# Latent attention in four quarters of four heads, woven between the projections of the next quarter

## The reference

```python
def mla(h, w_in, q_norm, w_q_up, kv_norm, w_kv_up, w_o):
    B, S, _ = h.shape
    lat = h @ w_in                                   # 384 + 256 + 32 columns
    cq = lat[..., :Q_LORA]
    ckv = lat[..., Q_LORA:Q_LORA + KV_LORA]
    k_rope = lat[..., Q_LORA + KV_LORA:][:, :, None, :]
    q = (rmsnorm(cq, q_norm) @ w_q_up).reshape(B, S, MLA_HEADS, QK_NOPE + QK_ROPE)    # 16 heads of 64 + 32
    kv = (rmsnorm(ckv, kv_norm) @ w_kv_up).reshape(B, S, MLA_HEADS, QK_NOPE + V_HEAD) # 16 heads of 64 + 64
    pos = jnp.arange(S, dtype=jnp.float32)
    q = jnp.concatenate([q[..., :QK_NOPE], rope(q[..., QK_NOPE:], pos)], axis=-1)
    k_rope = jnp.broadcast_to(rope(k_rope, pos), (B, S, MLA_HEADS, QK_ROPE))
    k = jnp.concatenate([kv[..., :QK_NOPE], k_rope.astype(kv.dtype)], axis=-1)
    v = kv[..., QK_NOPE:]
    o = causal_block_attention(q, k, v, (QK_NOPE + QK_ROPE) ** -0.5)
    return o.reshape(B, S, MLA_HEADS * V_HEAD) @ w_o
```

## Time and profile before

| what | value |
|---|---|
| median of 3 runs | 4606.94 us (4595.18 to 4607.84) |
| profiled execution, its time and span | 4603.62 us, 4601.8 us |
| TensorE busy | 4149.3 us, 90% of the span |
| VectorE, ScalarE, GpSimd busy | 50%, 28%, 18% |
| granted TensorE clock, mean | 0.91 |
| chain that ended last | PE 84%, DVE 11%, ACT 3%, issue 2% |

### The profile page before, as it was taken

The page is one execution under the profiler, slowest core; times in us unless marked ns, Lnnn a source line. Parts: engine busy times, 40 slices in busy tenths (PEclk is TensorE's granted clock), DMA queues, the critical chain, the costliest instruction groups (busy, mean ns, idle before and its releaser), DMA issues.

```text
span 4601.8 us, 50066 instructions
## 1 busy us (share of the span) xinstructions
PE 4149.3 (90%) x20156; PEld 3325.7 (72%) x20156; DVE 2298.0 (50%) x3067; ACT 1278.5 (28%) x1698; POOL 848.2 (18%) x580
## 2 busy tenths in 40 slices
PE   6885799997759999999877899999999999999998
PEld 5744688885457887888644788878877777777886
DVE  4546555564565555555354543453354444445334
ACT  3231223222313223222333322232233232232222
POOL 2300244541004554565201220000000000000000
PEclk8877899996869999999778899989989999998999
DMA  4200144430004444454101233323322121112331
GB/s 141 83 1 1 55 137 142 147 123 28 1 1 124 138 149 126 138 148 133 53 14 42 55 96 92 92 80 94 101 65 76 60 72 51 62 49 64 101 92 64
DMA packets 538850, 378.37 MB, mean 82 GB/s; under 512 B 8938, under 2 KB 536267, under 8 KB 538619
## 3 DMA queue, kind: packets, MB, share of 16 engines
q1 hardware_dynamic: 538042, 373.07, 27.3%
q10 hardware_dynamic: 576, 2.10, 0.1%
HBM read 372.96 MB, written 2.17 MB: 82 GB/s over the span
## 4 chain that ended last, share of the span: by engine, by line
PE 84%; DVE 11%; ACT 3%; issue 2%; SPq 0%; DMA 0%; DVEq 0%; ACTq 0%
PE bank L433 55%; PE bank L477 6%; PE bank L755 3%; PE bank L447 3%; PE bank L775 3%; PE bank L535 2%; PE bank L1204 2%; DVE w_lo L412 2%; PE bank L1598 1%; PE bank L1623 1%; PE bank L765 1%; DVE hgrn_scores L1137 1%; ACT w_hi L403 1%; PE bank L1643 1%; PE bank L554 1%
## 5 line engine op out<-in xcount | busy, mean ns | idle before, releaser
L433 PE MATMUL bank<-H_hi,w_hi 128*128 128x512 f32 (+1 forms) x2368 | 955.3, 403 | 6.1 <-DVE w_lo L412 5.9
L412 DVE TENSOR_TENSOR w_lo<-w_raw,w_hi 128x2048 fp32r<-128x2048 f32 (+2 forms) x281 | 730.2, 2599 | 439.3 <-ACT w_hi L403 432.5
L433 PE MATMUL bank<-H_lo,w_hi 128*128 128x512 f32 (+1 forms) x2368 | 927.1, 392 | 0.0
L433 PE MATMUL bank<-H_hi,w_lo 128*128 128x512 f32 (+1 forms) x2368 | 926.5, 391 | 0.0
L403 ACT ACTIVATE w_hi<-w_raw 128x2048 fp32r<-128x2048 f32 (+2 forms) x281 | 528.3, 1880 | 321.0 <-DMA w_raw<-in_ffn_w_up 148.4
L433 PE MATMUL bank<-U_hi,w_hi 128*128 128x512 f32 x1440 | 568.2, 395 | 8.2 <-DVE U_lo L1188 6.1
L433 PE MATMUL bank<-U_lo,w_hi 128*128 128x512 f32 x1440 | 563.3, 391 | 0.0
L433 PE MATMUL bank<-U_hi,w_lo 128*128 128x512 f32 x1440 | 562.6, 391 | 0.0
L433 PEld LDWEIGHTS bank<-H_hi,w_hi 128*128 128x128 f32 (+1 forms) x2368 | 446.4, 189 | 117.7 <-issue 21.5
L433 PEld LDWEIGHTS bank<-H_hi,w_lo 128*128 128x128 f32 (+1 forms) x2368 | 446.1, 188 | 96.2
L433 PEld LDWEIGHTS bank<-H_lo,w_hi 128*128 128x128 f32 (+1 forms) x2368 | 446.9, 189 | 89.4 <-issue 3.9
(11 more groups left out here) (288 smaller groups left out, 5319.8 us busy)
## 6 DMA issues: line engine op xcount, KB each, us to landing
w_mod_raw<-in_w_mod SPq DMA_DIRECT2D x144, 512.0 KB, 6.3
w_raw<-in_ffn_w_gate SPq DMA_DIRECT2D x88, 512.0 KB, 3.9
w_raw<-in_ffn_w_up SPq DMA_DIRECT2D x88, 512.0 KB, 5.2
w_raw<-in_dil_w_in SPq DMA_DIRECT2D x36, 1024.0 KB, 4.9
w_raw<-in_w_mlp_in SPq DMA_DIRECT2D x32, 1024.0 KB, 6.3
w_raw<-in_w_mlp_out SPq DMA_DIRECT2D x32, 1024.0 KB, 5.4
w_raw<-in_ffn_w_down SPq DMA_DIRECT2D x32, 1024.0 KB, 5.2
w_raw<-in_w_in SPq DMA_DIRECT2D x16, 1024.0 KB, 5.3
```

The costliest lines, as they stand in the source:

```text
L412: dve.eng.tensor_tensor(WL[u % SLOTS][:, 0:n], RAW[u % SLOTS][:, 0:n], WH[u % SLOTS][:, 0:n].bitcast(F32), ALU.subtract).then_inc(lo_done. ...
L433: mm = pe.eng.matmul(bank[0:m, :], w[:, k, c0:c0 + m], r[:, k, :], start=(k == 0 and i == 0), stop=(k == kt - 1 and i == 2))
```

## The change

The sixteen heads are done in four quarters of four heads. The weights of a quarter are loaded by head parts, with the 64 plain features of its four heads together and then the 32 rotated ones (or the values), so a query unit has three tiles of 128 rows (two with plain features of two heads each, one with the rotated features of four heads), and a key/value unit two tiles of keys and two of values (256 columns for each of two blocks of tokens). The rotation works on that tile of four heads at once: one swap product and two multiplications of 128 rows, and four additions into the four heads' query tiles.

An item may now hold several blocks of queries in one bank: a head has three items, of blocks 0 and 2 (128 + 384 keys), 3 (512) and 1 (256). The barriers are gone. In `mla_pe` the quarters' projections (two units) have 17 points, three projection products apart (six of 256 columns for the values), at which the attention steps of the quarter before, the norm and rotation of the keys (in the first quarter) and the query rotation (point 12) are issued; the last quarter's attention stands at 18 points in mla_out's first two units. All three engines walk through the same list of points; ScalarE takes projections out at the points of `MLA_EVACS`, and both splits of the unit two ahead stand at points 8 and 16. The query latents are normed inside mla_in's third unit. Banks 0 to 2 take the projections' sums; bank 3 holds the heads' results. The other attentions keep their order, with the steps in functions of their own.

```diff
-    for base in (0, 64):
+    for base in (0, 32, 64, 96):
...
+        def add_units(stage, rhs, specs, waits="tiles", acc=(0, 1, 2, 3)):
...
+                for part in range(4):
+                    q = wq[:, 4 * QK * part:4 * QK * (part + 1)].rearrange("r (h c) -> r h c", c=QK)
+                    kv = wkv[:, 4 * P * part:4 * P * (part + 1)].rearrange("r (h c) -> r h c", c=P)
+                    add_units(("mla_q", part), cq, [([(0, q[:, :, 0:NOPE]), (4 * NOPE, q[:, :, NOPE:QK])], 3, 4 * QK,
+                                                     [feat(0, P), feat(P, P), feat(2 * P, P)])], "none" if part else "tiles", acc=(0, 1, 2))
+                    add_units(("mla_kv", part), ckv, [([(0, kv[:, :, 0:NOPE]), (4 * NOPE, kv[:, :, NOPE:P])], 2, 4 * P,
+                                                       [feat(0, P), feat(P, P), tok(2 * P, 2 * P, [0, 1]), tok(2 * P, 2 * P, [2, 3])])],
+                              "none" if part else "tiles", acc=(0, 1, 2))
+                add_units(("mla_out",), U, [square(io["mla_w_o_2"][0], D, 256 * n) for n in range(4)])
...
+        def pe_pair(pe, u, weave=None, beside=4):
...
+            for together in (todo[:beside],) + ((todo[beside:],) if beside < 4 else ()):
+                for _, _, _, place, turn in together:
+                    pe.eng.wait_ge(acc_free[place].sem, turn - 1)
+                for k in range(kt):
+                    if together[0] is todo[0]:
+                        pe.eng.wait_ge(rhs_ready.sem, rhs_ready.next(pe))
...
+        def mla_slot(h):
+            return (h + 4) % 8
...
+        def mla_items(part):
+            items = []
+            for h in range(4 * part, 4 * part + 4):
+                s = mla_slot(h)
+                stat = 0
+                for blocks in ((0, 2), (3,), (1,)):
+                    segs, vals, c0 = [], [], 0
+                    for b in blocks:
+                        w = (b + 1) * P
+                        segs.append((MQ[0:QK, s, b * P:(b + 1) * P], MK[0:QK, s, 0:w], c0, CAUSAL))
+                        vals += [(MV[:, kb, s * HEAD:(s + 1) * HEAD], b * P, kb == 0, kb == b) for kb in range(b + 1)]
+                        c0 += w
+                    items.append({"segs": segs, "n": c0, "scale": QK ** -0.5, "stat": h * NB + stat, "row": HEAD * (h % 2), "v": vals,
+                                  "opens": h % 2 == 0 and blocks[0] == 0, "closes": h // 2 if h % 2 == 1 and blocks[0] == 1 else None})
+                    stat += len(blocks)
+            return items
...
+        MLA_POINTS = 17
+
+        def mla_steps(part):
+            if part == 0:
+                return []
+            n, out = 12, []
+            for s in range(n + 2):
+                if s < n:
+                    out.append(("scores", s))
+                if 1 <= s < n + 1:
+                    out += [("divide", s - 1), ("turn", s - 1)]
+                if s >= 2:
+                    out.append(("values", s - 2))
+            return out
+
+        def mla_at(part, points=MLA_POINTS):
+            todo = mla_steps(part)
+            where = [[] for _ in range(points)]
+            for j, step in enumerate(todo):
+                where[(2 * j + 1) * points // (2 * len(todo))].append(step)
+            if part == 0:
+                where[1].append(("latent_sums", 0))
+                where[4].append(("latent_spread", 0))
+                where[6].append(("key_swap", 0))
+                where[9].append(("key_rows", 0))
+            if part < 4:
+                where[12].append(("query_rope", part))
+            return where
+
+        MLA_EVACS = {2: ("mla_q", 0), 5: ("mla_q", 1), 8: ("mla_q", 2), 10: ("mla_kv", 0), 12: ("mla_kv", 1), 14: ("mla_kv", 2), 16: ("mla_kv", 3)}
...
+            elif kind == "query_rope":
+                sem, n = mla_last(("mla_q", part), 0, 2)
+                pe.eng.wait_ge(sem, n)
+                pe.eng.wait_ge(turn_used.sem, turn_used.next(pe, lag=1))
+                pe.eng.wait_ge(pt_ready.sem, pt_ready.taken["pe"])
+                pe.eng.matmul(banks[6][:], MSWAP, MR[:], start=True, stop=True).then_inc(turn_mm.sem, turn_mm.add())
+            else:
+                if kind == "scores" and i == 0:
+                    pe.eng.wait_ge(mla_ready.sem, mla_ready.next(pe))
+                    sem, n = mla_last(("mla_kv", part - 1), 0, 3)
+                    pe.eng.wait_ge(sem, n)
+                    if part == 1:
+                        pe.eng.wait_ge(key_rows.sem, key_rows.next(pe, 8))
+                if kind == "turn":
...
+        def mla_pe(pe):
+            first = lin[("mla_in",)][0]
+            pe_pair(pe, first)
+            beside = iter([None] * 5 + ["sums"] + [None] * 4 + ["spread"] + [None] * 5)
+
+            def latents():
+                what = next(beside)
+                if what == "sums":
+                    pe_sums(pe, 3, NT[0:2])
+                elif what == "spread":
+                    pe_spread(pe)
+            pe_unit(pe, first + 2, latents)
+            for part in range(5):
+                items = mla_items(part - 1) if part else []
+                where = iter(mla_at(part, MLA_POINTS if part < 4 else 18))
+
+                def weave():
+                    for step in next(where):
+                        mla_pe_step(pe, part, items, step)
+                if part < 4:
+                    pe_unit(pe, lin[("mla_q", part)][0], weave)
+                    pe_unit(pe, lin[("mla_kv", part)][0], weave)
+                else:
+                    pe_pair(pe, lin[("mla_out",)][0], weave, 3)
+                    for u in lin[("mla_out",)][2:]:
+                        pe_unit(pe, u)
...
+        def mla_act(act):
...
+            for part in range(5):
+                items = mla_items(part - 1) if part else []
+                for p, steps_ in enumerate(mla_at(part, MLA_POINTS if part < 4 else 18)):
+                    if part < 4 and p in MLA_EVACS:
+                        stage, j = MLA_EVACS[p]
+                        mla_evac(act, part, stage, j)
+                        if p in (8, 16):
...
+                if part == 0:
+                    act.eng.wait_ge(mla_rows.sem, mla_rows.next(act))
+                    for h in range(8):
+                        ae.activation(MK[NOPE:QK, h, :], MK0[NOPE:QK, :], ACT.Copy).then_inc(key_rows.sem, key_rows.add())
+                        act.eng.wait_ge(key_rows.sem, key_rows.made)
...
+            elif kind == "query_rope":
...
+                ve.tensor_tensor(MT[0][:], MR[:], COS[:], ALU.mult).then_inc(dve.step.sem, dve.step.add())
...
+                ve.tensor_tensor(MT[1][:], banks[6][:], SIN[:], ALU.mult).then_inc(turn_used.sem, turn_used.add())
...
+                for j in range(4):
+                    r = slice(ROPE * j, ROPE * j + ROPE)
+                    signal = mla_ready if j == 3 else dve.step
+                    ve.tensor_tensor(MQ[NOPE:QK, s + j, :], MT[0][r, :], MT[1][r, :], ALU.add).then_inc(signal.sem, signal.add())
+                    dve.eng.wait_ge(signal.sem, signal.made)
...
+                    if part < 4 and p in (8, 16):
+                        split_lo(dve, lin[(MLA_EVACS[p][0], part)][0] + AHEAD)
+                    for step in steps_:
...
+                    if len(src.shape) == 3:
+                        h, w = src.shape[1:]
+                        for k in range(kt):
+                            eng.dma_start(dst[:, k, c:c + h * w].rearrange("p (h w) -> p h w", w=w), src[k * P:(k + 1) * P]).then_inc(landed[s].sem, landed[s].add(16))
+                        continue
```

413 lines of the change are left out of this document (191 added, 222 removed).

## The result

The changed kernel took 4576.06 us (median of 5 runs), the kernel before beside it 4601.12 us (5 runs). The ratio is 0.9934, 95% interval 0.9922 to 0.9947: 24 to 36 us faster, outside the noise. The forecast was 4590 us, 17 us faster; it has the sign, the measured time lies inside its range of 4550 to 4626, and the gain is short by about 8 us (by the medians) to 13 us (by the ratio).

The account below looks back on a forecast made before the run. TensorE, busy 90% of the span, bounds the kernel, which gains where it waits or runs at low clock. 52 us gained at full clock, less 7, 7 and 21, leaves 17: 4606.94 - 17 = 4590 us, range 4550 to 4626.

Parts of the forecast that it names:

- switching: Latent attention, changes between full precision products and the projections': 0.1 us each, 17 per quarter, 7 us lost in all.
- GpSimd: Modulation columns computed on GpSimd now fall into the latent attention and slow operations there: 7 us lost, bounds 0 and 11.
- step 2: First quarter: projections, swap products, sums and spread, waits for the norm, first scores' wait for key rows: 31.2 us.
- step 3: Three quarters with attention, 69.5 us each, plus 0.6 for a table load and 3.8 for mla_out's split: 212.9 us.
- step 4: Last quarter's attention with mla_out's first 54 products, 60.1 us, then mla_out's other 138 products, 31.6 us.
- The added wait: Latent attention, turn one item nearer: TensorE waits for VectorE's maximum and division after each score product, 24.8 us per quarter.
- The clock: TensorE's clock halves for a while behind long waits in the quarters: 21 us lost, taken between 18 and 40.
- The swap product: Query rotation on TensorE: one product of 1.93 us for four heads, 7.7 us in place of 58.8 us of stretch.
- step 1: mla_in's third unit with the query norm inside: queries' projections start at 2237.3 us, not 2266, 28.7 us gained.
- The clock's rival: Clock stays down in the quarters: at 60% of them at 1.2 GHz, a quarter takes 88 us, 4627 us; chance 22%.
- Halved waits: Rival: TensorE's waits before turns are half the sum, 12 us less per quarter, fewer clock drops: 4545 us; chance 23%.
- late weights: Rival: small weight rows load slowly, 7 us late first, then 3 us for each of 8 units: 4607 us; chance 10%.

Follow-up runs that it names:

- no_weave: Changed kernel with all attention steps of a quarter at its first point, no projections between scores and turn: 4636.29 us, ratio 1.0075 to the kernel before.

## Why the prediction was right, and where it was not

The sum at full clock put the stage at 352.1 us (2573.1 - 2221.0). The kernel with its waits filled, at 0.96 to 1.00 in the quarters, took 351.1. That the two agree to 1 us is in part luck: the 14 us that the forecast took off for switching and GpSimd lie outside the sum, and its steps miss by 2 to 6 us in both directions. By its steps (step 2 begins with the first latent product, step 3 with the first scores, step 4 where the fourth quarter's products end):

| step | forecast at full clock, us | changed kernel, us | with products in the waits, us |
|---|---|---|---|
| 1, pair to first latent product | 16.3 | 18.3 | 18.3 |
| 2, first quarter with the wait for key rows | 31.2 | 27.8 | 27.8 |
| 3, second to fourth quarter | 212.9 | 228.6 (clock 0.82 to 0.90) | 207.8 |
| 4, last attention and mla_out | 91.7 | 97.6 | 97.2 |
| switching, GpSimd, clock | 35 | in the rows above | in the rows above |

- The added wait, the core of the forecast, was right item by item, and in its sum: 91.7 us forecast for the stage (three times 24.8, and 17.3), 82.1 before the turn and 3.8 for copies measured. Forecast for a quarter: 2.0, 1.0, 2.0, 1.5, 1.0, 2.0, 2.8, 1.9, 1.3, 4.3, 1.0, 4.0. Second quarter: 1.66, 0.84, 1.91, 1.39, 0.88, 1.91, 4.08, 1.54, 1.21, 4.85, 0.86, 0.98. Two failed. The twelfth was put at 4.0 for the keys' split; VectorE does that split at 2341.06 us, behind the last division, and what is left is a wait for a copy. The seventh was put at 2.8 and took 4.08, 3.43 and 5.36; without GpSimd's work it took 2.12, 2.12 and 4.13 (the last with the larger split of mla_out's weights).
- The clock: 21 us forecast, 21 in the stage and 25 by the medians. The 21 was picked between bounds of 18 and 40, so that it was hit so closely is luck. All of it lies in step 3 (228.6 against 207.8).
- GpSimd: 7 us forecast, 17 measured by the medians (13.5 in the stage). This is the mis-sized term: its price was read from one operation's length, while most of it comes through the clock behind the longer wait.
- The swap product was mis-sized too. The forecast took 1.93 us from the earlier trace rows into a sum at full clock, but that row stands in a stretch with a clock of 0.54. In the kernel after a swap takes 1.0 us (2324.19, 1.02). That is 2.8 of the 3.4 us by which the first quarter was shorter than forecast, and nearly 1 us in each of the next three.
- Why the total was 8 to 13 us too careful all the same: the clock and GpSimd were added, though they overlap; of the twelfth wait some 8 us over three quarters did not come, and 3.4 us of the first quarter. Against that, step 1 was 2 us and step 4 some 6 us too short. The waits of the last attention are as forecast (17.4 against 17.3 us) and it took as long with the waits filled, so what step 4 missed is neither; it stays open. The 0.1 us for a change of precision is there (2301.82 to 2302.14 is 0.32 us against 0.23), but no run measured its sum.
- The clock's rival (22%) did not come true in this kernel, and in no_weave it did: the same waits before the turn with no projections between, clock 0.66, slower than the kernel before. Halved waits and late weights are false (82.1 us of waits; plain columns made no difference).
- Of the signs: clock, length of a quarter and the places of the waits as forecast; TensorE busy 68 to 76%. Wrong: a quarter has eleven waits before a turn and not twelve; the longest one stands beside the query rotation (4.85 us) in the second and third quarter, but not in the fourth (5.36 at the seventh item); the first latent product starts at 2242.6 us, not at 2237, 3.5 us of it by the later start of the stage; the profile names no releaser for 44 waits; and outside the stage the times moved by 3.5 and 2.5 us, not by less than 2. Of the second, the norm behind mla_out now waits 2.95 us for a sum on VectorE in every kernel made from the changed one.
- What the forecast had not asked is what the change would bring with the old place of the turn. The answer is 103 us, of which the near turn takes back 78.

## What to carry to other kernels

When work is woven, keep one whole item between a division (or any other engine's answer) and the product that needs it; in these kernels a wait of 1 to 2 us per item was paid twice, once as idle time and again as half clock behind it. Price the clock from what TensorE does between the waits: the same 82 us of waits before the turn gave a clock of 0.82 to 0.95 with projections between, and 0.66 to 0.76 without. When a step is moved off a wait, look at what shares its bank and at what is due next, or the wait moves with it.

## What the runs showed that I had not expected

- Products whose result nobody reads made the kernel 25 us faster (4576 to 4551 us).
- With 62 waits of at most 1.9 us, 93 us together, the granted clock was 0.59 to 0.60 for 160 us on end, and TensorE's busy time for the same products rose from 74 to 110 us.
- Work off the path (GpSimd's multiplication and additions, 5 to 11 us busy in a quarter) was worth 17 us of the whole.
